# Moving the experts' two split token tiles from 32 to 192 bytes behind a multiple of 256

## What is computed

```python
gate, idx = lax.top_k(jnp.swapaxes(aff, 1, 2), cap)
xs = h[bidx, idx]
hid = jax.nn.silu(jnp.einsum('becd,edf->becf', xs, w1)) * jnp.einsum('becd,edf->becf', xs, w3)
y = jnp.einsum('becf,efd->becd', hid, w2) * gate[..., None].astype(h.dtype)
return jnp.zeros_like(h).at[bidx, idx].add(y)
```

## Time and profile before

| | |
|---|---|
| Median of 3 runs | 2159.51 us (2157.03 to 2159.64) |
| Profiled execution | 2155.37 us |
| Its span, first to last instruction | 2153.7 us |
| Matmuls busy | 2074.7 us, 96% of the span |
| VectorE busy | 1369.9 us, 64% |
| ScalarE busy | 996.1 us, 46% |
| Granted TensorE clock, mean | 0.988 of 2.4 GHz |
| One expert in the steady loop | 68.06 us |

### The profile page before, as it was taken

The page is one execution under the profiler, slowest core; times in us unless marked ns, Lnnn a source line. Parts: engine busy times, 40 slices in busy tenths (PEclk is TensorE's granted clock), DMA queues, the critical chain, the costliest instruction groups (busy, mean ns, idle before and its releaser), DMA issues.

```text
span 2153.7 us, 35092 instructions
## 1 busy us (share of the span) xinstructions
PE 2074.7 (96%) x13569; PEld 1815.5 (84%) x13569; DVE 1369.9 (64%) x2082; ACT 996.1 (46%) x1631; POOL 277.8 (13%) x357
## 2 busy tenths in 40 slices
PE   6999999999999899997999999999999999999996
PEld 4778888888878677785899999999999999999985
DVE  3664648995994577757555656556555665656557
ACT  5923454444531445431444544445444444445455
POOL 0001000100001010020011122111221112111120
PEclk9999999999999999998999999999999999999998
DMA  7463333333427665456357666576565765657565
GB/s 258 150 248 132 109 106 99 115 118 88 125 77 237 236 208 176 145 214 257 118 204 246 215 215 211 187 264 214 193 216 195 273 198 186 217 218 253 198 233 225
DMA packets 188285, 407.95 MB, mean 189 GB/s; under 512 B 15956, under 2 KB 53396, under 8 KB 187300
## 3 DMA queue, kind: packets, MB, share of 16 engines
q1 hardware_dynamic: 162212, 318.36, 42.6%
q0 software_dynamic: 25984, 88.39, 12.6%
HBM read 329.59 MB, written 77.12 MB: 189 GB/s over the span
## 4 chain that ended last, share of the span: by engine, by line
PE 80%; DVE 10%; ACT 3%; DMA 3%; issue 2%; SPq 1%; POOL 0%; DVEq 0%; ACTq 0%; POOLq 0%
PE bh L55 11%; PE bh L57 11%; PE bh L56 11%; PE bank L55 8%; PE bank L57 8%; PE bank L56 8%; PE eby L55 5%; PE eby L57 5%; PE eby L56 5%; DVE acc L854 3%; PE ebt L2283 1%; PE bank L1031 1%; DVE over L2012 1%; PE bank L1413 1%; DVE raw L2472 1%
## 5 line engine op out<-in xcount | busy, mean ns | idle before, releaser
L55 PE MATMUL bh<-xt_hi,shi 128*128 128x256 f32 x2048 | 572.2, 279 | 3.2 <-DVE slo L2436 2.7
L56 PE MATMUL bh<-xt_lo,shi 128*128 128x256 f32 x2048 | 571.6, 279 | 0.0
L57 PE MATMUL bh<-xt_hi,slo 128*128 128x256 f32 x2048 | 571.4, 279 | 0.0
L2436 DVE TENSOR_TENSOR slo<-raw,shi 128x1024 fp32r<-128x1024 f32 x384 | 456.0, 1221 | 156.9 <-ACT shi L2345 152.4
L2345 ACT ACTIVATE shi<-raw 128x1024 fp32r<-128x1024 f32 x384 | 389.8, 1052 | 127.1 <-PE eby L57 125.5
L55 PEld LDWEIGHTS bh<-xt_hi,shi 128*128 128x128 f32 x2048 | 385.3, 188 | 4.6 <-issue 2.5
L56 PEld LDWEIGHTS bh<-xt_lo,shi 128*128 128x128 f32 x2048 | 385.4, 188 | 0.6
L57 PEld LDWEIGHTS bh<-xt_hi,slo 128*128 128x128 f32 x2048 | 385.3, 188 | 0.0
L55 PE MATMUL bank<-h_hi,whi 128*128 128x512 f32 x704 | 283.4, 403 | 0.0
L57 PE MATMUL bank<-h_hi,wlo 128*128 128x512 f32 x704 | 275.4, 391 | 0.0
L56 PE MATMUL bank<-h_lo,whi 128*128 128x512 f32 x704 | 275.4, 391 | 0.0
(11 more groups left out here) (348 smaller groups left out, 3127.6 us busy)
## 6 DMA issues: line engine op xcount, KB each, us to landing
raw<-in_exp_w_dram SPq DMA_DIRECT2D x96, 2048.0 KB, 11.0
uT<-stage POOLq DMA_DIRECT2D x72, 256.0 KB, 2.7
xb<-in_ada_w_dram SPq DMA_DIRECT2D x24, 512.0 KB, 5.6
wraw<-in_w_in_dram SPq DMA_DIRECT2D x22, 512.0 KB, 5.4
adaw<-in_ada_w_dram SPq DMA_DIRECT2D x8, 1024.0 KB, 9.7
xb<-in_x_dram SPq DMA_DIRECT2D x16, 512.0 KB, 4.2
xt<-in_x_dram POOLq DMA_DIRECT2D x16, 512.0 KB, 5.3
x2d<-xt POOLq DMA_DIRECT2D x16, 512.0 KB, 3.0
```

The source lines that it names most:

```text
L55: nc.tensor.matmul(out, w_hi, x_hi, start=start, stop=False)
L56: nc.tensor.matmul(out, w_hi, x_lo, start=False, stop=False)
L57: return nc.tensor.matmul(out, w_lo, x_hi, start=False, stop=stop)
L2436: nc.vector.tensor_tensor(item_dst(slo, n), item_src(n), item_dst(shi, n), ALU.subtract).then_inc(S["w_lo_ready"], 1)
```

## The change

Two paddings in the layout change. The first, ahead of `xt_hi`, grows from 32 to 192 bytes, the second, behind `xt_lo`, shrinks from 224 to 64 bytes, so that `ht_hi` and all that comes behind it stay where they were. No instruction is added, removed or moved, no wait changes, and the sizes and types of all tiles are the same.

```diff
         xs = [t[:, :].bitcast(F32) for t in xs_words]
-        at[0] += 32
+        at[0] += 192
         xt_hi, xt_lo = sb("xt_hi", [P, KD, CAP], F32R), sb("xt_lo", [P, KD, CAP], F32R)
-        at[0] += 224
+        at[0] += 64
         ht_hi, ht_lo = sb("ht_hi", [P, FD, CAP], F32R), sb("ht_lo", [P, FD, CAP], F32R)
```

## The result

The changed kernel took 2159.95 us (median of 20 runs, 2156.88 to 2162.97), the kernel before 2155.29 us (median of 20 runs, 2153.34 to 2159.64; its first three are those shown ahead of the change). The ratio is 1.0021, with a 95% interval of 1.0015 to 1.0027. The forecast of 2138.6 us had the wrong sign. The 2159.5 us that it started from, the median of three runs, lay 4.2 us above the median of the twenty.

A forecast was written before the change was run, and what follows sets the result against it. TensorE's own stream of matmuls was taken to bound the experts' stage. 6144 up products at 113.2 instead of 116.6 ns gave -20.9 us, all other terms 0, so 2159.5 became 2138.6 us; range 2124 to 2183 us.

The forecast's parts named there:

- What bounds the kernel: Experts' stage: TensorE's matmuls run one behind another, so the pitch of 6144 up products, 116.6 ns each, goes whole into the time.
- The row at 0 as the price of place 0: Up products: the context projection's 120.0 ns, moving tile at 0, taken as place 0's pitch; upper bound of +20.9 us.
- From 0 and 32 to 192, by distance: Up products: 192 is two 32-byte steps from the next 0, worth 6.8 ns; pitch 113.2 ns, -20.9 us.
- One place, one pitch: Up products: the tile's place taken as cause of the pitch, 116.6 ns at 32, read in one expert.
- The base and the range: Whole kernel: start from 2159.5 us; range 2124 to 2183 us, leaving out the deepest gain and worst loss, 0.20 together.
- the likeliest case: Up products: two steps of distance, 2138.6 us, own range 2124 to 2150 us; chance 0.31.
- The case of no effect: Up products: the place doesn't matter, or any place but 0 serves alike; 116.6 ns, 2159.5 us; chance 0.28.
- back to the pitch of 0: Up products: 192 lies on the memory's grid like 0; 120.0 ns, +20.9 us, 2180.4 us; chance 0.21.
- grid of 64 bytes: Up products: interleave repeats within 64 bytes, so 0, 64, 128 and 192 are alike; 3.4 ns per product lost.
- the streams never meet: Up products: 64 bytes or more apart, weights and tokens never collide; 108.9 ns, -47 us, 2112 us; chance 0.12.
- The writers, the turn, the down products, the cover: Beside the up products: each taken as 0, writers at most 0.5 us either way; VectorE and the weight transfers keep up.
- The rule of two read ports: TensorE: the skill's independent read ports for moving operand and weight load mean place can't matter; time stays 2159.5 us.

The follow-up runs named there:

- place0: Both token tiles at 0, all else as in the kernel before: 2174.2 us in one execution, beside 2154.5 us for the kernel before.
- near: Kernel of matmuls alone: weights at four places, tokens 0, 32 or 192 bytes further on, then bfloat16 operands; 120.0 ns at equal places, 109.3 ns for bfloat16.
- flat192: Changed kernel plus TensorE's wait for its last down product ahead of each expert but the first, its loop written out: 2141.85 us, 0.9932 of the kernel before.
- relock192: Changed kernel plus TensorE's wait for its own last down product ahead of each expert but the first, loop kept: 2167.1 us, 1.0049 of the kernel before.
- late192: Changed kernel plus the same wait as relock192, placed directly ahead of the first up product: 2167.3 us, 1.0054 of the kernel before.
- flat192_free: Changed kernel with TensorE's loop written out and no wait added: 2160.7 us, 1.0029 of the kernel before.
- relock32: Kernel before (tiles at 32) plus TensorE's wait for its own last down product ahead of each expert but the first: 2167.1 us, 1.0045 of the kernel before.

## Why the prediction was wrong, point by point

- **What bounds the kernel: right.** The up products lie on the path to the end without cover. The pitch times the number of products gives the time of the loop: 3.3 ns more at place 0 made 17.8 us more in its 14 experts, and the kernel took 20 us more.
- **The row at 0 as the price of place 0: right.** It was called an inference from two rows; `place0` and the equal places of `near` showed it, and the distance between weights and tokens as its cause.
- **From 0 and 32 to 192, by distance: wrong, and this is the step that failed.** "One step was worth 3.4 ns, so two are worth 6.8" made a line through two points, folded it at 128 and read it at 192. The runs show no such line: 120.0, 116.7, 117.8, 120.1, 120.0, 118.6, 117.8, 118.3 ns for 0 to 224 behind down products. By chance the forecast's 113.2 ns is the pitch of expert 0, of 384 of the 6144 products. 117.8 ns in the rest is 1.1 ns above the old pitch and not 3.4 below.
- **One place, one pitch: wrong, and the trace of before already had the sign of it.** The pitch was read in expert 7 and in no other. Its expert 0 runs the same products on the same places at 117.8 ns. Whoever read both would have known that the place doesn't set the pitch alone, and that a row at another place bounds less than it seems.
- **The base and the range.** That 2159.95 us agrees with the 2159.5 us from which the forecast started is chance, since the base was 4.2 us high: the change is +4.7 us. It also lies inside the range of 2124 to 2183 us, which says little of the working, since the range spans both signs. The range's lower end doesn't follow from its own words either: the likeliest case with half as much gain again is 2159.5 - 31.4 = 2128 us.
- **The rivals.** The case of no effect was nearest in size, but its mechanism isn't what happened: the ratio of 1.0021 (1.0015 to 1.0027) is clear of 1, though not told apart from the 0.2% that was set as its border, and the pitch moved both ways within one execution. The case "back to the pitch of 0" had the right sign, with 3.4 ns per product where the loop paid 1.1 ns, and 20.9 us where the time rose by 4.7; its grid of 64 bytes fell with place 0, at 120.0 ns where 64 has 117.8. The case "the streams never meet" was not reached by any float32r run.
- **The writers, the turn, the down products, the cover: right.** The turn's and down products' pitches did not move, VectorE and ScalarE are busy for 40.6 and 31.9 us per expert, to 0.1 us as before, and even at 67.1 us per expert in `flat192` TensorE is not held up by them.
- **The rule of two read ports.** The page "TensorE: Matmul & The Clock Gate" of the Trainium skill says in "Step-by-step: what each phase is for" that loading the next weights takes no read bandwidth from the running matmul. The bfloat16 rows, 109.3 ns at all four places, fit it. For float32r the pitch of the same matmuls goes from 113.3 to 120.0 ns with nothing but the distance of the two operands and the start of the run, so here it doesn't hold as a statement on the time. Which resource the two operands share isn't shown.

What stays open: what in the start of a run picks the lock. It isn't a wait as such (`relock192`'s loop), nor the gap from the first to the second matmul (`late192`), nor code written out as such (`flat192_free`), nor a wait and written-out code together (`late192`'s expert 15), and `relock32` changed locks between one pass of its loop and the next. That two streams share the memory and meet in turns is argued from the distance, the four-byte condition and the repeating patterns; no view shows a meeting. Nor is it shown that the pattern repeats after 256 bytes: distances from 0 to 224 were tried, and of those beyond only the down products' operands are an odd multiple of 256 bytes apart, with the surplus of distance 0.

## What to carry to other kernels

Where back-to-back float32r matmuls bound a kernel, the byte distance between stationary and moving tiles is worth a few per cent of their time; it isn't monotonic and isn't to be interpolated, but a kernel of matmuls alone maps all places in one run, and reproduced what the loop had at each of the six tried, if the same kind of work ran ahead of the up products. It did not reproduce expert 0. Read the pitch in every pass of a loop and not in one: if it differs between passes, how a run begins is a second knob, and a wait that costs 0.3 us can give 1.7 us back. Leave the first knob alone when the second is not under control: 192 is the best place of all here with it and worse than 32 without.

## What the runs showed of the hardware that was not expected

- The pitch of a long run is constant, but its steps repeat: at 192 in the slow lock from 117 to 119 ns, on average 117.8. In columns of 1/2.4 ns the commonest means come out as whole or third numbers: 113.3 ns is 272 columns, 116.7 is 280, 120.0 is 288, 117.8 is 848 / 3 over the three matmuls of a product; 256 of them are the columns themselves. The surplus is then 16, 24 and 32 columns, and 262 in all for bfloat16.
- The surplus of a float32r matmul is the same for 256 and for 512 columns, 13.3 ns with both operands at 0 (120.0 and 226.7 ns against 106.7 and 213.3; 226.7 is the down products' pitch once a run has settled, the 226.9 above takes in two slower steps near its start). So it is paid per matmul and not per column. That the weight load beside it is the reason is argued and not shown.
- A lock held through all 384 products in each of experts 0 to 14. It changed only from one expert to the next, or at a wait for weights inside expert 15 (116.7 to 117.8 ns there in the kernel before).
